# A hybrid decoder layer on one core: loads and small steps at the borders of stages in another order

## The reference

```python
h += W_out . concat[PoolMixer(u), SSD(z, xBC, dt)]   # [u|z|xBC|dt] = RMSNorm(h) . W_in
h += W2 . relu(W1 . RMSNorm(h))^2
out = RMSNorm(h)                                     # the meta positions are dropped
```

## Time and profile before

| | us |
|---|---|
| median of 3 runs | 2904.22 |
| lowest and highest | 2899.64, 2907.06 |
| the profiled execution, its own time | 2906.24 |
| its span, first to last instruction | 2904.4 |
| TensorE, VectorE, ScalarE, GpSimd busy in it | 2813.1, 1698.4, 1310.0, 1482.6 |
| mean granted TensorE clock | 0.986 |

### The profile page before, as it was taken

How to read it: one execution, slowest core, us unless ns; L and a number is a source line. 1 busy time by engine, 2 the same in 40 slices (tenths; PEclk the granted TensorE clock), 3 DMA queues, 4 the chain that set the end, 5 groups by cost and what they waited for, 6 DMA issues and landing times.

```text
span 2904.4 us, 35702 instructions
## 1 busy us (share of the span) xinstructions
PE 2813.1 (97%) x13310; PEld 2309.0 (79%) x13310; DVE 1698.4 (58%) x2173; ACT 1310.0 (45%) x2244; POOL 1482.6 (51%) x955
## 2 busy tenths in 40 slices
PE   8999999999999999999999999999999799999998
PEld 6688877888778887878877778877888688888887
DVE  4577723777427775157773546655444466667667
ACT  2355534555446554365552544454445322222223
POOL 1365543555445554446555657766555435343433
PEclk9999999999999999999999999999999899999999
DMA  8322133422234222342213346555444742333323
GB/s 239 102 73 66 53 115 109 131 70 62 95 109 138 67 72 80 99 156 73 66 59 131 123 167 218 188 186 177 144 153 170 301 159 102 145 116 131 109 102 145
DMA packets 289290, 363.03 MB, mean 125 GB/s; under 512 B 8906, under 2 KB 214350, under 8 KB 280030
## 3 DMA queue, kind: packets, MB, share of 16 engines
q1 hardware_dynamic: 289118, 360.75, 37.4%
HBM read 272.64 MB, written 88.08 MB: 124 GB/s over the span
## 4 chain that ended last, share of the span: by engine, by line
PE 90%; POOL 2%; DVE 2%; issue 1%; DMA 1%; ACT 1%; DVEq 0%; SPq 0%; ACTq 0%; POOLq 0%
PE bank L1616 26%; PE bank L1899 20%; PE bank L1867 20%; PE bank L1641 11%; PE bank L1723 2%; PE bank L1728 2%; PE bank L1707 1%; PE bank L1691 1%; PE bank L1737 1%; PE bank L1675 1%; PE bank L1699 1%; PE bank L1680 1%; POOL w_lo L434 1%; PE bank L1713 1%; DMA third<-T_scr 1%
## 5 line engine op out<-in xcount | busy, mean ns | idle before, releaser
L434 POOL TENSOR_TENSOR w_lo<-raw,w_hi 128x1024 fp32r<-128x1024 f32 x208 | 506.8, 2437 | 657.2 <-ACT w_hi L426 657.2
L426 ACT ACTIVATE w_hi<-raw 128x1024 fp32r<-128x1024 f32 x208 | 220.0, 1058 | 575.5 <-PE bank L1616 333.8
L1616 PE MATMUL bank<-hnT_hi,w_hi 128*128 128x512 f32 x1152 | 462.6, 402 | 3.5 <-ACT pre L1260 3.5
L1616 PE MATMUL bank<-hnT_hi,w_lo 128*128 128x512 f32 x1152 | 450.3, 391 | 0.0
L1616 PE MATMUL bank<-hnT_lo,w_hi 128*128 128x512 f32 x1152 | 449.7, 390 | 0.0
L1921 DVE SCALAR_TENSOR_TENSOR acc<-pre,par,acc 128x512 f32<-128x512 f32 x240 | 251.6, 1048 | 120.9 <-ACT pre L1260 114.8
L1899 PE MATMUL bank<-w_first,T_hi 128*128 128x512 f32 x896 | 275.9, 389 | 0.4 <-DVE T_lo L2205 0.4
L1616 PEld LDWEIGHTS bank<-hnT_hi,w_hi 128*128 128x128 f32 x1152 | 217.1, 188 | 46.5 <-issue 4.4
L1616 PEld LDWEIGHTS bank<-hnT_hi,w_lo 128*128 128x128 f32 x1152 | 216.5, 188 | 46.7
L1616 PEld LDWEIGHTS bank<-hnT_lo,w_hi 128*128 128x128 f32 x1152 | 217.2, 189 | 41.9
L2223 DVE TENSOR_TENSOR acc_th<-bank,acc_th 128x512 f32<-128x512 f32 x224 | 150.2, 686 | 160.6 <-PE bank L1899 160.4
(11 more groups left out here) (296 smaller groups left out, 6248.0 us busy)
## 6 DMA issues: line engine op xcount, KB each, us to landing
raw<-in_w_in SPq DMA_DIRECT2D x168, 512.0 KB, 3.9
T_scr<-stage SPq DMA_DIRECT2D x32, 1792.0 KB, 6.7
pair_raw<-in_w_ff SPq DMA_DIRECT2D x36, 1024.0 KB, 5.4
raw<-in_w_out SPq DMA_DIRECT2D x64, 512.0 KB, 3.5
third<-T_scr SPq DMA_DIRECT2D x28, 1024.0 KB, 4.8
pair_raw<-T_scr SPq DMA_DIRECT2D x28, 1024.0 KB, 4.8
w_raw<-in_w_ff SPq DMA_DIRECT2D x12, 1024.0 KB, 8.4
h<-in_x SPq DMA_DIRECT2D x5, 2048.0 KB, 10.8
```

What stands on the lines that cost most here:

```text
L426: nc.scalar.activation(w_hi[:, N % 2, :], raw[:, N % RING, :], ACT.Copy).then_inc(w_hi_ready, 1)
L434: nc.gpsimd.tensor_tensor(w_lo[:, N % 2, :], raw[:, N % RING, :], w_hi[:, N % 2, :].bitcast(F32), ALU.subtract).then_inc(w_lo_ready, 1)
L1616: mm = nc.tensor.matmul(bank[s][:, :], w[:, k, :], t[:, k, :], start=(k == 0 and j == 0), stop=(k == KT - 1 and j == 2))
```

## The change

Five edits, all of order or place. In the blocks' first units, the scaling of the stream goes ahead of unit 0, the root for it ahead of the low part, and the transposes one unit earlier. In the last head group `finish` of the pooling unit before goes behind `yo`. At the end of the last block the four quarters are loaded in a row, GpSimd's sums and ScalarE's high parts are placed at earlier units, and two low parts instead of one stand ahead of the first `down_sum`. `hT_last` is split in two pieces at other addresses, stored by two DMAs, and the wait for them moves from ScalarE's `relu_square` to VectorE's `t_sums` of pair 1. At the start of the second feed-forward stage the loads are ordered anew. The diff, with its smallest follow-ups left out:

```diff
-        hT_last = at("hT_last", [P, KT, TB], R0 + 47104)
+        hT_last = [at("hT_last0", [P, 5, TB], R0 + 61440), at("hT_last1", [P, 3, TB], R0 + 49152)]
...
-        RIGHT_HIGH_AT = {(0, 6): 0, (1, 0): 1, (1, 1): 2, (1, 2): 3, (1, 3): 4, (1, 4): 5, (1, 6): 6}
+        RIGHT_HIGH_AT = {(0, 4): 0, (0, 6): 1, (0, 7): 2, (1, 0): 3, (1, 2): 4, (1, 4): 5, (1, 6): 6}
...
                                 hT_stored.wait(sp, 1, 16)
-                                load_quarter(0)
-                                load_quarter(1)
-                            if b == LAST and (d, i) in ((0, 7), (1, 0)):
-                                load_quarter(2 + d)
+                                for k in range(4):
+                                    load_quarter(k)
...
                     if p == 2:
                         hT_ready.wait(sp, LAST, KT)
-                        sp.dma_start(hT_scr[LAST], hT_last[:, :, :]).then_inc(hT_stored.sem, 16)
+                        sp.dma_start(hT_scr[LAST, :, 0:5, :], hT_last[0][:, :, :]
+                                     ).then_inc(hT_stored.sem, 16)
+                        sp.dma_start(hT_scr[LAST, :, 5:KT, :], hT_last[1][:, :, :]
+                                     ).then_inc(hT_stored.sem, 16)
...
-                for half in range(2):
-                    for t in range(CH):
-                        acc_load(0, half, t)
-                        if (half, t) == (0, 3):
-                            sp.wait_ge(T_stored[0], 16 * PAIRS)
-                            w2_load(1)
+                for t in range(CH):
+                    acc_load(0, 0, t)
+                sp.wait_ge(T_stored[0], 16 * PAIRS)
+                w2_load(1)
                 sp.wait_ge(prod1, PRODS)
                 w2_load(2)
+                for t in range(CH):
+                    acc_load(0, 1, t)
+                t_load(2)
                 store_pair(2 * PAIRS - 1)
-                t_load(2)
-                for half in range(2):
-                    for t in range(CH):
-                        acc_load(1, half, t)
-                sp.wait_ge(T_stored[1], 16 * PAIRS)
-                w2_load(3)
-                w2_load(4)
                 for x in range(1, STEPS2):
                     t_load(x + 2)
                     q, half = divmod(x, 2)
                     c, i = divmod(q, 7)
+                    if x in (1, 2):
+                        for t in range(CH):
+                            acc_load(1, x - 1, t)
+                    if x == 3:
+                        sp.wait_ge(T_stored[1], 16 * PAIRS)
+                        w2_load(3)
+                        w2_load(4)
...
                     for n in range(UNITS_G):
-                        low_part(pool, N0 + n + 2)
                         if b and n == 0:
                             inverse_root(b - 1, r2[:, :], ssf[:, :], h_sumsq, CH, h_rstd, CH)
+                        low_part(pool, N0 + n + 2)
...
-                                name = {(0, 6): "t1", (0, 7): "t2", (1, 1): "t3", (1, 3): "t4"
+                                name = {(0, 4): "t1", (0, 5): "t2", (0, 6): "t3", (1, 1): "t4"
                                         }.get((d, u))
...
+                    if b:
+                        for t in range(CH):
+                            h_scale(b - 1, t)
                     for n in range(UNITS_G):
                         high_part(act, N0 + n + 2)
                         evac(b, n)
...
-                        if b and n < 2:
-                            h_scale(b - 1, 2 * n)
-                            h_scale(b - 1, 2 * n + 1)
-                        if b and 2 <= n < 6:
-                            for k in (2 * n - 4, 2 * n - 3):
-                                h_tile(b - 1, k, hT, bank[2 + k % 2][:, :])
+                        if b and 1 <= n < 5:
+                            for k in (2 * n - 2, 2 * n - 1):
+                                h_tile(b - 1, k, hT[:, k, :], bank[2 + k % 2][:, :])
...
                         dst = stage[:, p % 2, pos, :]
-                        if p == 1:
-                            hT_stored.wait(act, LAST, 16)
...
                         unit(b, n)
-                        if b and 2 <= n < 6:
-
-                            for k in (2 * n - 4, 2 * n - 3):
+                        if b and 1 <= n < 5:
+
+                            for k in (2 * n - 2, 2 * n - 1):
...
-                        if c:
+                        if c and n1 is not None:
                             finish(b, pending)
                         finish(b, n1)
...
                                                 per_head(ea, c, g), ALU.mult
                                                 ).then_inc(yo_ready.sem, 1)
+                        if c and n1 is None:
+                            finish(b, pending)
                         taps(b, n2)
                         if q:
                             y_low(b, q - 1)
...
                     if b == LAST:
                         right_low(0)
+                        right_low(1)
                     down_sum(b, 0)
                     if b == LAST:
-                        for i in range(1, 7):
+                        for i in range(2, 7):
                             right_low(i)
...
                     dve.wait_ge(sq_done, 4 * p + 4)
+                    if p == 1:
+                        hT_stored.wait(dve, LAST, 32)
```

More of the change, by code:

```diff
@@ L930, in bg_load @@
                     else:
-                        hT_stored.wait(sp, LAST, 16)
+                        hT_stored.wait(sp, LAST, 32)
                     for s, name in enumerate(QUARTERS):
@@ L1287, in h_tile @@
                     hT_ps.wait(act, b, k + 1)
-                    nc.scalar.activation(dst[:, k, :], src, ACT.Copy,
+                    nc.scalar.activation(dst, src, ACT.Copy,
                                          scale=par[:, W_NFFN + k:W_NFFN + k + 1]
@@ L1582, in _ @@
                         for k in (2 * g - 10, 2 * g - 9):
-                            h_tile(LAST, k, hT_last, bank[6 + k % 2][:, :])
+                            h_tile(LAST, k, hT_last[k // 5][:, k % 5, :], bank[6 + k % 2][:, :])
                     n = {0: 4 * p - 1, 3: 4 * p, 5: 4 * p + 1, 6: 4 * p + 2}.get(i)
```

## The result

| | before | after |
|---|---|---|
| median, us (4 runs each) | 2905.64 | 2947.03 |
| lowest and highest | 2899.64, 2909.71 | 2946.72, 2952.18 |
| ratio, 95% interval | | 1.0147 (1.0134 to 1.016) |
| profiled execution, own time and span | 2906.24, 2904.4 | 2947.19, 2945.5 |
| mean granted TensorE clock | 0.986 | 0.985 |

A forecast was written before the change was run, and what follows sets the result against it. TensorE, busy 97% of the span, was taken as the bound. From 2906.2 us, -4.5 + 52 + 2 - 9.4 - 4.5 gave 2941.8, taken as 2940 beside the median; range 2908 to 2964 for 8 in 10.

The forecast's parts named there:

- Part 2: Last head group, four blocks: pooling behind `yo` takes turns with GpSimd, `y_low` comes late; 13.0 us a block, 52 lost.
- The clock term: Part 2, each block: three spells of low TensorE clock for one old spell, 2.4 us more.
- Part 1: Start of blocks 1 to 3: stream scaled early, 1.8 us wait for `h` goes; gain 4.5 us (0 to 5.3).
- Part 3: Last block's output projection: first bank free 5.3 us late, partly regained later; loss 2 us (-3 to +8).
- Part 4: First feed-forward stage: 7.0 us wait behind the store of `hT_last` goes, 2.4 of clock too; gain 9.4 us (5 to 10).
- Part 5: Second feed-forward stage: load of T step 2 goes ahead of a 1.84 MB store; gain 4.5 us (2 to 9).
- A: Rival on part 2: GpSimd lets VectorE through, so it gives 8 us instead of costing 52; 2880 us, chance 0.12.
- B: Rival on part 2: the waits come, but VectorE wins two of GpSimd's turns, 30 us less; 2910 us, chance 0.08.
- C: Rival: all new waits bring the long spell of low clock and part 3 costs 8 us; 2963 us, chance 0.12.
- D: Rival: gains of parts 4 and 5 don't come, store or quarters only change places in the queue; 2954 us, chance 0.08.

The follow-up runs named there:

- both narrow kernels: Part 2 alone on the kernel before, with VectorE's pooling operations, or GpSimd's three operations in the last head group, on 32 columns: 2933.72 and 2898.8 us.
- the run with L1943 first: The change without part 2, with `finish` of the unit before put ahead of the softplus steps in units 2 to 4: 2881.2 us, 0.9915 of the kernel before.
- The two kernels of the gains together: The change without part 2, L1943 ahead of softplus steps, last step's pooling behind `state_add`: 2867.85 us with part 3, 2866.31 with it undone.

## Why the prediction was right, and where it wasn't

**Part 2 (forecast +52, measured +51.1).** The step that carried it, that VectorE's pooling and GpSimd's three operations take strict turns, held in each operation, and both narrow kernels confirm it. The waits of block 1 were to be 4.0, 4.7 and 4.4 us and are 3.7, 4.4 and 4.1: each forecast 0.3 too long. The removed wait was 2.5. That is 9.7 us of idle time where 10.6 were forecast. The clock term was put at 2.4 and is 2.8 by what is left of block 1's 12.5. The three stretches behind the new waits in the changed kernel (columns as above):

```profile
748.20:751.70 3.50, 3.50 (x14) 3.02 (x13) 2.59 (x5) 1.75 (x5) 0.93 (x3) 0.52 0.00 0
764.20:771.10 6.90, 6.90 (x26) 5.89 (x27) 3.22 (x6) 2.21 (x5) 1.96 (x3) 0.66 0.00 0
782.50:786.10 3.60, 3.26 (x8) 2.62 (x9) 3.43 (x8) 0.62 (x2) 1.10 (x2) 0.53 0.24 92
```

They cost 0.48 x 3.5 = 1.7, 0.34 x 6.9 = 2.3 and 0.47 x 3.6 = 1.7 us, and the spell of before that went had cost 3.1; 5.7 - 3.1 = 2.6. The two errors have opposite signs, so the sum came closer than its terms, which is luck. Block 0 has 14.3, since the spell that went there was a short one. Alone, part 2 costs 55.8 by the marks, 4.7 more than by its places in the changed kernel; 3.9 of these are the shorter spell of 3.4 us, which the change had without part 2 too.

**Part 1 (forecast -4.5, measured +4.3 at its place).** This is the step that failed: "The scaling ends early, so I take 0.3 us. Gain 1.5 x 3 = 4.5 us (0 to 5.3)". The gain is real, the run with L1943 first has it. What was left out is what an earlier TensorE triggers: GpSimd's low part follows it and moves up by 0.65 us against the block's start, a product of VectorE that had begun 0.3 us ahead of it by only 0.1, and the order of the two is turned. The bounds excluded a loss with no reason given. The rows for it were in the trace of before (494.62 beside 494.94, shown above), and the look for such a collision was made in the paragraph on part 2. With 8.8 us this is the largest miss of the five; the others took some 3 us back from it, which leaves the profiled execution's 2947.2 for a sum of 2941.8.

**Part 3 (+2, measured +1.5)** was sized by how late the projection's second half starts, 5.3 us, and that is 5.1; what comes back behind it is 3.6. Of the 5.1 the new wait for `w_lo` is 1.8 and the wait for `h`, 4.7 instead of 3.3, is 1.4. Its explanation was too narrow: it blamed `right_low(1)`, and without that GpSimd's sums bind. **Part 4 (-9.4, measured -9.6)** held in both terms. **Part 5 (-4.5, measured -6.0)** had 4.9 us of it in the wait of L1899, but the size came out by luck in part. The forecast gave it all to the 1.84 MB that the load no longer stands behind. In the run of part 5 alone, where the wait is 5.1 us shorter, the load is in flight for 14.00 us instead of 17.06, 3.1 less; the other 2 come from its earlier issue (2275.54 instead of 2278.05, with the whole kernel 0.4 earlier): it no longer stands in SyncE's program behind a store that waits for VectorE's last sums. The last 1.1 of the changed kernel are clock, which the term left out: the slow spell outlasts the wait by 3.2 us instead of 5.5.

**The rivals.** A (GpSimd lets VectorE through) fell by 2.34 us for a copy of 0.17. B (VectorE wins two turns) fell, as no turn was won after the first copy. C fell: of the twelve slow spells behind the new waits nine were short (3.4 us) and three long (6.8). D fell, parts 4 and 5 came. The Trainium skill ("SBUF — State Buffer", section "SBUF: two separate sides") has an exclusive lock on ports that VectorE and GpSimd share: whichever starts first keeps them for its whole instruction, and VectorE needs them for operations with two inputs in SBUF, the memory of the tiles. The trace agrees. The operations held up have their inputs there (the copies, with one input, are held up too); those with one input in PSUM, TensorE's banks, are not slowed. The profile of the changed kernel has both kinds, L1921 at a mean of 1038 ns where it takes 740 to 750 alone, and L2228, with a bank as input, at 686, of which 95 of 224 fall on GpSimd's work, with the same 0.69 us as the others:

```profile
L1921 DVE SCALAR_TENSOR_TENSOR acc<-pre,par,acc 128x512 f32<-128x512 f32 x240 | 249.2, 1038 | 119.2 <-ACT pre L1262 113.0
...
L2228 DVE TENSOR_TENSOR acc_th<-bank,acc_th 128x512 f32<-128x512 f32 x224 | 150.5, 686 | 168.9 <-PE bank L1899 168.7
```

## What to carry to other kernels

A chain of small VectorE operations beside GpSimd's work is priced more by how many operations GpSimd has queued than by the chain's width (29 of 53 us stayed at a sixteenth of the width): put such a chain where nobody waits for what is behind it, and put the one operation that others wait for first. When a step is made earlier, look for what every engine behind it then starts earlier, and by how much each: a few tenths of a microsecond decide where VectorE and GpSimd hold each other up. Where only one step of a loop has the late operation, move that step alone, and behind all that is waited for: it gained 12.9 us, where the move right behind `yo` in all steps cost 53.

## What the runs showed of the hardware

- A copy of 16 columns (0.17 us alone) takes 2.34 us and an operation on 96 columns (0.26 alone) 2.50 when it begins behind a GpSimd low part of 2.4 us. The smallest operations pay the most for their size. In steps 13 to 15 the turns alternate strictly: between two GpSimd operations one of VectorE's was let in, never two.
- Which engine is hit is decided by 0.3 us: with VectorE 0.32 ahead, GpSimd's operation takes 2.64 instead of 2.40 and VectorE's 0.69; with GpSimd 0.25 ahead, VectorE's takes 2.77.
- Slow spells of TensorE (granted clock 0.50) followed waits of 3.7 and 4.1 us with a length of 3.4 us, and one of 6.8 us began 2.2 us ahead of the end of the wait of 4.4. The two kernels of the gains together have 44.5 us (part 3 undone) and 51.8 us (with it) of slow clock in all, the one before 85.3, the changed one 93.1.
- The same wait of 2.5 us for `yo` went with a slow spell of 6.8 us in blocks 1 to 3 of the kernel before and of 3.4 us in those of four others, the ones that scale the stream early and keep this wait; no run tells why. The same wait for `w_lo` (L1641), in nine kernels whose last projection is that of the kernel before, is 2.3 to 2.8 us in four profiled executions and 3.9 to 4.0 in five, in no relation to the edit. A term of 2 us needs more than one profile.
